# Projection in units of 512 columns, with four modulation slots among the first layer's projection slots

## What is computed

```
for l in range(2):
    m = silu(cvec) @ w_ada[l] + b_ada[l]           # 1024 x 6144: shift, scale and gate of both halves
    h = rmsnorm(x, norm1_g[l]) * (1 + sc1) + sh1
    qa, ka, va, ub, qc, kc, vc = split(h @ w_in[l]) # widths 512, 512, 512, 512, 512, 128, 128
    oA = differential attention(rope(qa), rope(ka) + cached keys, va + cached values)
    oB = pooling of ub over 2, 4, 8, 16 tokens, then w_pool
    oC = windowed attention(rope(qc), rope(kc) + cached keys, vc + cached values)
    x  = x + g1 * (sum of sigmoid(h @ w_gate) * (o @ w_branch)) @ w_out[l]
    h2 = rmsnorm(x, norm2_g[l]) * (1 + sc2) + sh2
    x  = x + g2 * (dense SwiGLU for l = 0, top 2 of 8 experts for l = 1)(h2)
y = rmsnorm(x, final_g);   ka, va, kc, vc of the prompt are outputs too
```

## Time and profile before

| what | us |
|---|---|
| median of 3 runs (1619.73 to 1624.29) | 1623.38 |
| the profiled execution | 1622.29 |
| its span, first to last instruction | 1619.9 |
| PE busy in it | 1515.3 (94%) |
| DVE busy | 955.6 (59%) |
| ACT busy | 783.3 (48%) |
| mean granted clock of TensorE | 0.971 of full speed |

### The profile page before, as it was taken

How to read it: one execution, slowest core, us unless ns; L and a number is a source line. 1 busy time by engine, 2 the same in 40 slices (tenths; PEclk the granted TensorE clock), 3 DMA queues, 4 the chain that set the end, 5 groups by cost and what they waited for, 6 DMA issues and landing times.

```text
span 1619.9 us, 23720 instructions
## 1 busy us (share of the span) xinstructions
PE 1515.3 (94%) x9317; PEld 1365.2 (84%) x9317; DVE 955.6 (59%) x1199; ACT 783.3 (48%) x899; POOL 48.8 (3%) x55
## 2 busy tenths in 40 slices
PE   5799989999989999997999999999899999999993
PEld 3799958769989999997999787798788888888883
DVE  2552345463654345435533564546788988888887
ACT  3433335263342233224334453534677787777873
POOL 1000000000000000001000000000000000000020
PEclk8899999999989999997999999999999999999997
DMA  9853366374423344252443453534699999999993
GB/s 325 322 187 114 104 217 217 127 255 148 130 80 116 125 135 130 103 161 93 135 135 110 157 182 130 162 129 169 217 369 369 375 373 368 363 367 371 381 382 132
DMA packets 246985, 342.83 MB, mean 212 GB/s; under 512 B 8709, under 2 KB 178350, under 8 KB 246654
## 3 DMA queue, kind: packets, MB, share of 16 engines
q1 hardware_dynamic: 237632, 313.32, 57.2%
q0 software_dynamic: 6640, 25.21, 4.1%
q10 hardware_dynamic: 2638, 3.24, 0.6%
HBM read 325.74 MB, written 16.00 MB: 211 GB/s over the span
## 4 chain that ended last, share of the span: by engine, by line
PE 83%; DMA 5%; DVE 5%; ACT 4%; issue 1%; ACTq 0%; SPq 0%; DVEq 0%; POOLq 0%
PE ps L586 25%; PE ps L588 24%; PE ps L587 24%; PE ps L757 2%; DMA raw<-in_w_ada_dram 2%; DMA raw<-in_w_in_dram 2%; PE ps L601 1%; PE ps L725 1%; DVE wlo L1752 1%; PE ps L742 1%; ACT whi L1290 1%; DVE wlo L1457 1%; PE ps L940 1%; PE ps L654 1%; ACT whi L1083 1%
## 5 line engine op out<-in xcount | busy, mean ns | idle before, releaser
L586 PE MATMUL ps<-hhi,whi 128*128 128x384 f32 x864 | 292.2, 338 | 5.2 <-DVE hlo L1491 4.4
L588 PE MATMUL ps<-hhi,wlo 128*128 128x384 f32 x864 | 289.3, 335 | 0.0
L587 PE MATMUL ps<-hlo,whi 128*128 128x384 f32 x864 | 289.2, 335 | 0.0
L1457 DVE TENSOR_TENSOR wlo<-raw,whi 128x2048 fp32r<-128x2048 f32 x66 | 151.1, 2290 | 161.9 <-ACT whi L1083 161.6
L1752 DVE TENSOR_TENSOR wlo<-raw,whi 128x2048 fp32r<-128x2048 f32 (+1 forms) x81 | 180.6, 2231 | 36.7 <-ACT whi L1290 35.7
L1290 ACT ACTIVATE whi<-raw 128x2048 fp32r<-128x2048 f32 (+1 forms) x81 | 151.6, 1871 | 56.4 <-PE ps L588 56.2
L1752 DVE TENSOR_TENSOR wlo<-mraw,whi 128x2048 fp32r<-128x2048 f32 (+2 forms) x81 | 160.8, 1993 | 22.4 <-ACT whi L1290 22.4
L586 PE MATMUL ps<-whi,xgh 128*128 128x512 f32 (+1 forms) x432 | 165.0, 382 | 8.8 <-DVE wlo L1752 6.8
L586 PEld LDWEIGHTS ps<-hhi,whi 128*128 128x128 f32 x864 | 162.8, 188 | 8.7 <-issue 6.2
L586 PE MATMUL ps<-whi,hhi 128*128 128x256 f32 x528 | 154.2, 292 | 11.3 <-DVE hlo L1491 11.3
L587 PEld LDWEIGHTS ps<-hlo,whi 128*128 128x128 f32 x864 | 162.8, 188 | 0.6
(11 more groups left out here) (295 smaller groups left out, 2558.7 us busy)
## 6 DMA issues: line engine op xcount, KB each, us to landing
raw<-in_w_ada_dram SPq DMA_DIRECT2D x86, 512.0 KB, 5.3
raw<-in_w_ex_up_dram SPq DMA_DIRECT2D x27, 1024.0 KB, 7.0
raw<-in_w_ex_down_dram SPq DMA_DIRECT2D x27, 1024.0 KB, 7.7
raw<-in_w_gate_dram SPq DMA_DIRECT2D x48, 512.0 KB, 4.5
raw<-in_w_in_dram SPq DMA_DIRECT2D x44, 512.0 KB, 5.0
raw<-in_w_ex_gate_dram SPq DMA_DIRECT2D x18, 1024.0 KB, 5.5
mraw<-in_w_ex_gate_dram SPq DMA_DIRECT2D x18, 1024.0 KB, 7.8
mraw<-in_w_ex_down_dram SPq DMA_DIRECT2D x18, 1024.0 KB, 7.3
```

The costliest lines, as they stand in the source:

```text
L586: pe.matmul(out, s[0], m[0], start=first, stop=False, **kw)
L587: pe.matmul(out, s[0], m[1], start=False, stop=False, **kw)
L588: return pe.matmul(out, s[1], m[0], start=False, stop=last, **kw)
L1457: dve.tensor_tensor(wlo[:, n % RING, :], raw[:, n % RING, :], whi[:, n % RING, :].bitcast(F32), ALU.subtract).then_inc(lo_done, 1)
```

## The change

The projection is done in six units, `PROJ` in place of `WIN`: four of queries, keys, values and pool inputs of 512 columns and two slots each (a slot now is 512 rows by 512 columns), one more of 512 for the window queries, and one of 256 columns in one slot for the window keys and values. A unit of 512 runs its first slot over all three blocks and then its second; units take banks 0 to 2 and 3 to 5 in turn. Each block of a unit has its own semaphore step, so that ACT copies it out while PE is at the next block. `stage` is one buffer of 512 columns a block. A unit's two turnings stand after the second and the third block of the next unit's first slot, in banks that this unit does not use. Phase 1 of the modulation has four slots, after projection slots 2, 4, 6 and 8; the first attention of layer 0 has nine in place of twelve; that of the second attention stands at steps 1 to 10 in place of 0 to 9. Key and value outputs leave in four transfers a layer. `gate_pair` gives the two bank pairs of the gates in the other order.

```diff
-ADA_SLOTS = (8, 1, 12, 12, 8, 7)
+ADA_SLOTS = (8, 4, 9, 12, 8, 7)
...
-ADA_STEPS = {2: (0, 1, 2, 3, 4, 5, 6, 7, 8, 11), 3: tuple(range(10)), 4: (1, 3, 5, 7, 9, 11), 5: (1, 3, 5, 7, 9)}
+ADA_STEPS = {2: (1, 2, 4, 5, 7, 8, 11), 3: tuple(range(1, 11)), 4: (1, 3, 5, 7, 9, 11), 5: (1, 3, 5, 7, 9)}
...
-WIN = (0, 1, 2, 3, 8, 9, 10, 4, 5, 6, 7)
-N_ROT = 7
+PROJ = ((0, 512), (512, 512), (2048, 512), (2560, 256), (1024, 512), (1536, 512))
+Q_A, K_A, Q_C, KV_C, V_A, U_B = range(len(PROJ))
+PROJ_SLOTS = ((0, 1), (2, 3), (4, 5), (6,), (7, 8), (9, 10))
+N_ROT = 4
...
-            return (n - gate_slot(l, 0, 0, 0) + 1) % 2
+            return (n - gate_slot(l, 0, 0, 0)) % 2
...
+        def proj_out(u):
+
+            return ps[:, 3 * (u % 2):3 * (u % 2) + 3, 0:PROJ[u][1]]
+
+        def turned_banks(ti):
+
+            if ti % 2 == 0:
+                return (0, 1) if ti in (0, 4) else (3, 4)
+            return (2, 6) if ti in (1, 5) else (5, 6)
...
+            def projection_slot(l, s):
+
+                u = [s in x for x in PROJ_SLOTS].index(True)
+                c0, width = PROJ[u]
+                if u == KV_C:
+                    k_by_cols(win_slot(l, s), a["w_in"][l], KD, c0, width)
+                else:
+                    k_by_cols(win_slot(l, s), a["w_in"][l, 512 * PROJ_SLOTS[u].index(s):][0:512], 4, c0, width)
...
-                    if l == 0 and s == 3:
-                        modulation(1)
-                    k_by_cols(win_slot(l, s), a["w_in"][l], KD, 256 * WIN[s], 256)
+                    if l == 0 and s in (3, 5, 7, 9):
+                        modulation(1, ((s - 3) // 2,))
+                    projection_slot(l, s)
...
             def input_projection(l):
...
                 for p in range(4):
                     pe.wait_ge(h_ready, 8 * l + p + 1)
+                    if p % 2 == 0:
+                        pe.wait_ge(lo_done, split_count(win_slot(l, p // 2) + 1))
+                    for b in range(BLK):
+                        mm = products(Q_A, b, (2 * p, 2 * p + 1))
...
+                for u in range(1, len(PROJ)):
+                    if u > 1:
+                        pe.wait_ge(win_evac, evac_turn(l, u - 2, 2) if u - 2 != KV_C else evac_turn(l, KV_C, 1))
+                        pe.wait_ge(tr_evac, N_TR * l + (2 * (u - 1) if u < U_B else N_TR))
+                    for i, s in enumerate(PROJ_SLOTS[u]):
+                        pe.wait_ge(lo_done, split_count(win_slot(l, s) + 1))
+                        for b in range(BLK):
+                            mm = products(u, b, range(4 * i, 4 * i + 4) if u != KV_C else range(KD))
+                            if b == BLK - 1:
+                                mm.then_inc(mm_done, 1)
+                            elif i == 1:
+                                mm.then_inc(proj_block, 1)
+                            if i == 0 and b and u <= V_A:
+                                ti = 2 * (u - 1) + b - 1
+                                if ti < N_TR - 1:
+                                    rot_transposes(l, ti)
+                                else:
+                                    context_transposes(l)
+                        if l == 0 and s in (2, 4, 6, 8):
+                            ada_product(1, s // 2 - 1)
+                        if l == 0 and s == 9:
+                            ada_end(1)
...
+            def input_evac(l, u):
+                out = proj_out(u)
+                if u <= KV_C and u:
+                    act.wait_ge(tr_done, N_TR * l + 2 * u)
...
+                for u, slots in enumerate(PROJ_SLOTS):
+                    if l:
+                        hi(win_slot(l, slots[0] + 2))
+                    if 1 <= u <= V_A:
+                        for ti in (2 * u - 2, 2 * u - 1):
+                            turned_evac(l, ti)
+                    if l == 0 and len(slots) == 2:
+                        hi(win_slot(l, slots[0] + 2))
+                    if l == 0 and u == U_B:
                         ada_rows(1)
                         ada_end(1)
+                    if l and len(slots) == 2:
+                        hi(win_slot(l, slots[1] + 2))
+                    input_evac(l, u)
+                    if l == 0:
+                        hi(win_slot(l, slots[-1] + 2))
```

More of the change, by code:

```diff
@@ L204, in prefix_step_kernel @@
         kTC = place("kTC", [2, 512])
-        stage = place("stage", [2, BLK, 256])
+        stage = place("stage", [BLK, 512])
         ctxv = place("ctxv", [640])
@@ L419, in unit_slot, with modulation @@
                     sp.dma_start(dst, src).then_inc(raw_in[j], 16)
-            def modulation(phase):
-                for i in range(ADA_SLOTS[phase]):
+            def modulation(phase, part=None):
+                for i in part or range(ADA_SLOTS[phase]):
                     l, c = divmod(ADA_AT[phase] + i, N_ADA // 2)
@@ L645, in rot_transposes @@
             def rot_transposes(l, ti):
[L647 to L651, removed]
+                pe.wait_ge(rope_done, N_ROT * l + ti // 2 + 1)
+                if ti % 2 and (l or ti > 1):
+                    pe.wait_ge(tr_evac, N_TR * l + ti - 1)
+                for c, bank in enumerate(turned_banks(ti)):
                     for b in range(BLK):
-                        src = kcd[:, b, c * P:(c + 1) * P] if ti == 6 else stage[:, ti % 2, b, c * P:(c + 1) * P]
-                        mm = pe.transpose(ps[:, 4 + c, b * P:(b + 1) * P], src, ident)
+                        x = 256 * (ti % 2) + c * P
+                        src = kcd[:, b, c * P:(c + 1) * P] if ti == 6 else stage[:, b, x:x + P]
+                        mm = pe.transpose(ps[:, bank, b * P:(b + 1) * P], src, ident)
@@ L655, in rot_transposes, with products @@
                 mm.then_inc(tr_done, 1)
             def input_projection(l):
[L658 to L666, removed]
+                def products(u, b, ks):
+                    s = PROJ_SLOTS[u][ks[0] // 4 if len(PROJ_SLOTS[u]) == 2 else 0]
+                    w = slot(win_slot(l, s), 4 if len(PROJ_SLOTS[u]) == 2 else KD)
+                    for k in ks:
+                        kw = k % 4 if len(PROJ_SLOTS[u]) == 2 else k
+                        mm = mm3(proj_out(u)[:, b, :], [h[:, k, b * P:(b + 1) * P] for h in (hhi, hlo)],
+                                 [x[:, kw, :] for x in w], k == 0, k == KD - 1)
+                    return mm
@@ L830, in branch @@
                         if o == half == 0:
-                            pe.wait_ge(win_evac, win_turn(l, 9 + j))
+                            pe.wait_ge(win_evac, evac_turn(l, V_A, 2) if j == 0 else evac_turn(l, U_B, 0))
                         if o and half == 0 and j == 0:
@@ L1127, in modulate @@
                         hi(win_slot(0, 1))
[L1129 to L1156, removed]
@@ L1882, in _ @@
                 normalise(2 * l, l > 0)
-                for s in range(N_WIN):
-                    lo(win_slot(l, s + 2))
-                    if s < N_ROT:
-                        rotate(l, s)
+                for u, slots in enumerate(PROJ_SLOTS):
+                    if l or len(slots) == 2:
+                        lo(win_slot(l, slots[0] + 2))
+                    if l and len(slots) == 2:
+                        lo(win_slot(l, slots[1] + 2))
+                    if u < N_ROT:
+                        rotate(l, u)
+                    if l == 0:
+                        lo(win_slot(l, slots[-1] + 2))
                 for o in range(3):
```

127 lines of the change are left out of this document (65 added, 62 removed).

## The result

The changed kernel took 1599.53 us (median of 4 runs, 1598.21 to 1601.91), the kernel before it, beside it, 1621.87 (4 runs, 1619.73 to 1624.29): a ratio of 0.9863, 95% interval 0.9843 to 0.9884. The forecast was 1601.0, with a range of 1595 to 1609. The profiled execution took 1600.18 us, with a span of 1598.5 against 1619.9.

What follows compares the result with a forecast made beforehand. PE, busy 94%, was taken to bound the kernel, with loads holding layer 0's first attention. Projections -5.7 and -7.4, attentions -7.5 and -1.4 gave -22.0 us: 1600.3 from the profiled 1622.29, 1601 against the median; range 1595 to 1609.

Steps and rivals of the forecast that it cites:

- Width: Both projections: 348 pairs of 256-column matmuls merged into 512s at 0.2267 us save 4.6 us a layer (3.2 to 8.0).
- The stalls: Projections: both waits for ACT's copy of turned queries and the low clock behind go, -4.3 us layer 0, -4.0 layer 1.
- What is late next: Projections: `V_A` waits for ACT's copies of the sixth turning, +1.2 us in layer 1, +0.2 in layer 0.
- The dear end: Projection, ahead of `V_A`: a lowered clock behind the wait could cost another 1.5 us.
- Rival A: Projection unit borders: new stalls for a turning or rotation, with low clock, 4.2 us a layer: 1609.5 us; chance 0.12.
- Three slots in the projection: Layer 0 projection: three more modulation slots cost 3.0 us of PE; their loads nothing, 4.5 us at the dear end.
- rival D: Layer 0 projection: PE idles for slot loads; over 0.3% slower needs the three to cost 27 us; chance 0.02.
- turnings: Projections: eight turnings of six transposes a layer at 0.65 us each, so 5.2 us stays.
- The first attention: Layer 0: nine slots for twelve take 32.3 us, 1.6 of it DMA wait for the fourth slot: -7.5 (-5.5 to -8.8).
- Rival B: Layer 0's first attention: PE late for loads at four of seven steps, about 1 us each: 1605.5 us; chance 0.08.
- The second attention: Layer 0: same slots one step later remove 1.4 us of load waits, to near 48.5 us: -1.4 (0 to -2.9).
- C: Projections: width saves little, as a 512-column matmul costs 0.238 us or so: 1608.5 us; chance 0.06.

Runs made afterwards that it cites:

- e1_halves: Changed kernel with each 512-column projection product done as two of 256: 1607.53 us, ratio 0.9918 to the kernel before.
- e4_first_turning_moved: Kernel before, with only its first turning moved behind the third window's second block and its copies ahead on ACT: 1613.58 us, ratio 0.9955.
- e2_old_split: Changed kernel with one modulation slot in layer 0's projection and twelve in the first attention, as before: 1605.70 us, ratio 0.9911 to the kernel before.
- e8: Changed kernel itself, run again on another chip: 1600.44 us, ratio 0.9854 to the kernel before.
- e3: Changed kernel with the slots of layer 0's second attention back at steps 0 to 9: 1603.61 us, ratio 0.9895 to the kernel before.
- e6: Changed kernel with `V_A` waiting for the sixth turning's copy only ahead of its third block: 1598.16 us, ratio 0.9838 to the kernel before.
- e5_fourth_slot_later: Changed kernel with first-attention slots at steps 1, 3, 5, 6, 7, 9, 11, the fourth one step later: 1598.58 us, ratio 0.9840 to the kernel before.

## Why the prediction was right, and where its sizes were off

**Width.** Forecast -4.6 a layer from a pace of 0.2267 us. The twelve starts of layer 1 shown above came out at 0.2267 too, and `e1_halves` gives 4.1 and 4.4. Not every stretch is as fast: in layer 0 twelve starts took 57.08 - 54.33 = 2.75 us, 0.2292 each. The DMA beside them isn't the reason, as the windows of the two stretches show:

```profile
54.33:57.08 2.75, 2.75 (x14) 2.25 (x12) 1.49 (x3) 2.24 (x2) 1.03 (x2) 1.00 0.61 232
...
766.90:769.62 2.72, 2.72 (x13) 2.25 (x12) 2.21 (x7) 1.61 (x2) 0.00 (x0) 1.00 1.03 397
```

The faster one has the DMA engines busy throughout. So had the 256s of the earlier trace rows, with a DMA share of 0.98 from 59.87 to 65.27. The prediction chose the line through the 256s and 384s because their stages were "as quiet as the projection". The pace that it got was right, but the reason isn't borne out, and what slows the 512s in some stretches (and in the experts, 0.2308) was not tried. The missing 0.2 to 0.5 us a layer stay open.

**The stalls.** Forecast -4.3 and -4.0, shown by `e4_first_turning_moved` as -4.7 and -3.8, or -4.1 in both with the clock at the start put right. This is the largest part of the gain in the projections, on a level with width.

**What is late next.** Forecast +1.2 ahead of `V_A` in layer 1, nothing but 0.2 in layer 0. The wait measured 1.0 and none, and taking it away gained 1.2. The dear end, a lowered clock behind it, didn't come: the clock is 1.00 in the 8 us from 796.65 on. Rival A (stalls at the borders) falls, as there is no other wait.

**Three slots in the projection.** Forecast +3.0 on PE and nothing for loads. No wait for a load stands in either projection, which is what rival D needed. The gap of 1.35 us in layer 0 (-4.35 for -5.7) is about the sum of small terms: width worth 0.5 less, the slots' 0.3 to 0.5 more in `e2_old_split`, 0.3 us more lost to the clock at the start (0.65 for 0.69 in the first 8 us), and turnings at 0.69 us for 0.65, eight times 0.04. (Twelve matmuls with one turning between them took 758.03 - 754.62 = 3.41 us in layer 1, less 12 x 0.2267.) They come to 1.4 to 1.6 us, but each is known only to one or two tenths, so that they meet the gap shows none of them singly.

**The first attention.** Here one term was mis-sized. The prediction had 32.3 us, with 1.6 of waiting for the fourth slot's load; the stage took 33.06 with 2.87. PE was ready at 219.34 - 2.87 = 216.47, 5.88 us after the stage's start (forecast 5.90). The load was issued 213.24 - 210.59 = 2.65 us after it, also as forecast. Only the time of the load was off, as the chain that ended last shows:

```profile
212.83 0.37 SPq L407
213.20 0.04 issue
213.24 6.06 DMA raw<-in_w_ada_dram
```

I had taken 4.87 us from a single row; it took 6.06 here and 5.40 in `e8`, where the wait was 2.2 us and the stage 32.14. The other executions with this order of slots lie between and beyond: waits of 1.6, 2.2 and 2.1 us for this load and 31.88, 32.75 and 33.43 us for the stage in `e1`, `e3` and `e6` (the last at a clock of 0.95). So 32.3 is inside the spread of one and the same order, and the -6.80 of the table could have come out at -6.4 to -8.0. A load on whose landing a whole term stands should have been taken from several rows, with their spread. `e5_fourth_slot_later` shows that the remainder of the stage was right: without this wait it is 31.00. Rival B (waits at four of seven steps) falls, with one such wait in the stage.

**The second attention.** Forecast 48.5 us and -1.4, measured 48.53 and -1.4, and the release by DVE as said. The 48.5 is firm, as six executions at full clock have it. The -1.4 is less so: against the 49.34 us of `e4_first_turning_moved`, which has the old steps, it would have been -0.8. And `e1_halves` and `e3_steps_back` show that the clock can move this stage by 1.6 us. It was luck that neither of the two executions compared had it lowered.

**The sum.** The terms gave -22.0 and the four stages -19.5. The forecast of the time was nearer than that (-22.3 by the medians), since 2 us more came from stages that it left alone, which no theory here accounts for: that closeness is luck. Of the rivals' prices, three are not what their own terms add up to (A: 1600.3 + 8.4 = 1608.7, not 1609.5; C: 1600.3 + 2 x 4 = 1608.3, not 1608.5; by a saving of 2.5 ns for a pair it would be 1607.8, not 1608.1). As these rivals fell, nothing hangs on it.

Not tried: the projection without POOL's fill beside it, and still more slots in it.

## What to carry to other kernels

Where PE bounds a stage, read the granted clock behind each of its stalls before pricing them: in the projections 2.3 and 2.9 us of waiting cost some 4 us each, and moving one turning got it back, while a wait of 2.87 us in the first attention left the clock at 1.00. Where loads bound the stage, a lower clock cost next to nothing: 39.86 us at 0.96 and 39.9 at 1.00. Loads that make a stage wait belong in a neighbouring stage that has DMA to spare, and the price was then little more than the engine's work: 2.3 to 2.5 us for 7.4. A merged matmul could be priced here from two streams of other widths in the same trace, to within 0.5 us of 4.6.

## What had not been expected of the hardware

The moment at which the clock rises in a projection differs between executions of the same work. In the first 8 us of layer 1's projection its mean was 0.64 in the changed kernel and in `e6`, and 0.75 in `e1_halves`, a difference of 0.9 us; over all ten profiled executions it ran from 0.62 to 0.77. Two readings of this stage are therefore to be compared only with their first window beside them.

The second attention of layer 0 ran at 1.00 in the changed kernel and at 0.91 over its first 9.8 us in `e1_halves`, with the same waits, at a cost of 1.6 us. A wait of 1.0 us ahead of `V_A` left the clock at 1.00, where waits of 2.3 and 2.9 us were followed by 0.57 and 0.59. The length of a wait alone doesn't decide it: the 2.87 us in the changed kernel's first attention were followed by 1.00, the 2.1 us of `e6` in the same place by 0.72 over the 6 us from 218 us on.

The load of 512 KB on which the first attention waits landed 4.87 us after its issue in the kernel before, 6.06 in the changed kernel and 5.40 in its second run, each time as the first transfer after a stretch with the DMA engines idle: a spread of 1.2 us on something that PE waits for. It isn't alone on its way: it is one of the two halves of its slot, and the next slot's halves are issued behind it. In the 6.06 us, 3.00 at 237 GB/s and 3.10 at 361, 1.8 MB were moved.
